# Gaps in the tile of split weights: weights that begin 192 bytes beyond the activations modulo 512

## What is computed

```python
def reference(x, ...):
    x = first_block(x, ln_pre_g, w_in, conv_w, conv_b, w_rg, b_rg, w_ig, b_ig, lru_lambda,
                    w_rnn_out, w_attn_out, w_o, ln_post_g)
    return second_block(x, g_pre_2, w_in_2, ...)

# first block, per layer
    h = rms_norm(x, ln_pre_g[layer])
    proj = jnp.einsum('bsd,de->bse', h, w_in[layer])
    ...
    y = jnp.einsum('bsd,de->bse', merged, w_o[layer])
    x = x + rms_norm(y, ln_post_g[layer])

# second block, per layer
    h = _rmsnorm(x, g_pre)
    u = h @ w_in
    ...
    for n in range(1, N_BRANCH):
        y = y + gates[:, :, n] * (branches[n] @ w_branch[n])
    return y @ w_out
```

## Time and profile before

| | |
|---|---|
| median of 3 runs | 3157.13 us (3156.27 to 3157.97) |
| profiled execution, span from the first to the last instruction | 3154.9 us |
| granted TensorE clock, mean | 0.998 |
| TensorE matmuls | 3134.1 us busy, 99% of the span, 18230 |
| TensorE weight loads | 2741.8 us, 87%, 18230 |
| VectorE | 2130.5 us, 68% |
| ScalarE | 1733.0 us, 55% |
| moved by DMA | 571.67 MB, mean 181 GB/s |

### The profile page before, as it was taken

The page is one execution under the profiler, slowest core; times in us unless marked ns, Lnnn a source line. Parts: engine busy times, 40 slices in busy tenths (PEclk is TensorE's granted clock), DMA queues, the critical chain, the costliest instruction groups (busy, mean ns, idle before and its releaser), DMA issues.

```text
span 3154.9 us, 52176 instructions
## 1 busy us (share of the span) xinstructions
PE 3134.1 (99%) x18230; PEld 2741.8 (87%) x18230; DVE 2130.5 (68%) x2741; ACT 1733.0 (55%) x2291; POOL 0.2 (0%) x4
## 2 busy tenths in 40 slices
PE   9999999999999999999999999999999999999999
PEld 7888888888888788888888888888888888888888
DVE  7677575666667687766666555777776666655575
ACT  5685444444445556656555555645665656555563
POOL 0000000000000000000000000000000000000000
PEclk9999999999999999999999999999999999999999
DMA  7656655555556555565556655566556565665555
GB/s 230 194 168 200 198 187 166 183 177 172 181 167 208 178 168 163 156 198 173 174 171 192 184 181 182 181 198 186 158 157 202 170 179 167 192 189 180 178 185 175
DMA packets 569809, 571.67 MB, mean 181 GB/s; under 512 B 26352, under 2 KB 565488, under 8 KB 569712
## 3 DMA queue, kind: packets, MB, share of 16 engines
q1 hardware_dynamic: 569712, 570.42, 58.9%
HBM read 568.25 MB, written 2.10 MB: 181 GB/s over the span
## 4 chain that ended last, share of the span: by engine, by line
PE 97%; DVE 1%; ACT 1%; DMA 0%; SPq 0%; issue 0%; ACTq 0%; DVEq 0%
PE pg L537 91%; PE pa L771 1%; PE pa L788 1%; PE pa L537 1%; PE pa L778 1%; PE pa L747 1%; PE pa L789 1%; DVE hl L1276 0%; PE pa L704 0%; DMA raw<-w_o 0%; PE pa L878 0%; DMA raw<-w_in 0%; ACT hl L933 0%; SPq L456 0%; DVE uT L1357 0%
## 5 line engine op out<-in xcount | busy, mean ns | idle before, releaser
L537 PE MATMUL pg<-hT,hl 128*128 128x512 f32 x11456 | 2030.6, 337 | 1.1 <-DVE hl L1276 1.1
L537 PEld LDWEIGHTS pg<-hT,hl 128*128 128x128 f32 x11456 | 1750.9, 188 | 261.1 <-DVE hl L1276 4.2
L1276 DVE TENSOR_TENSOR hl<-raw,hl 128x1024 fp32r<-128x1024 f32 (+1 forms) x1071 | 1256.0, 1209 | 314.5 <-ACT hl L933 306.8
L933 ACT ACTIVATE hl<-raw 128x1024 fp32r<-128x1024 f32 (+1 forms) x1071 | 1084.0, 1044 | 313.1 <-PE pg L537 293.8
L537 PE MATMUL pg<-uT,hl 128*128 128x256 f32 (+1 forms) x3712 | 639.1, 333 | 15.9 <-DVE uT L1357 7.5
L537 PEld LDWEIGHTS pg<-uT,hl 128*128 128x128 f32 x3712 | 558.4, 190 | 92.2 <-issue 14.2
L941 ACT ACTIVATE corr<-pg 128x512 f32<-128x512 f32 x286 | 170.3, 596 | 843.0 <-PE pg L537 843.0
L537 PE MATMUL pg<-hl,hT 128*128 128x256 f32 (+1 forms) x1792 | 317.9, 336 | 0.0
L1283 DVE TENSOR_TENSOR work<-pg,corr 128x512 f32<-128x512 f32 (+1 forms) x154 | 105.8, 687 | 303.7 <-ACT corr L941 303.5
L537 PEld LDWEIGHTS pg<-hl,hT 128*128 128x128 f32 x1792 | 274.9, 188 | 40.7
L1283 DVE TENSOR_TENSOR gat<-pg,corr 128x512 f32 (+1 forms) x71 | 48.9, 689 | 139.4 <-ACT corr L941 139.4
(11 more groups left out here) (191 smaller groups left out, 1369.2 us busy)
## 6 DMA issues: line engine op xcount, KB each, us to landing
raw<-w_in SPq DMA_DIRECT2D x791, 512.0 KB, 4.7
raw<-w_br SPq DMA_DIRECT2D x96, 512.0 KB, 4.3
raw<-w_out SPq DMA_DIRECT2D x64, 512.0 KB, 4.7
raw<-w_rnn SPq DMA_DIRECT2D x32, 512.0 KB, 4.8
raw<-w_o SPq DMA_DIRECT2D x32, 512.0 KB, 5.0
raw<-w_att SPq DMA_DIRECT2D x16, 512.0 KB, 4.4
raw<-w_uq SPq DMA_DIRECT2D x16, 384.0 KB, 4.0
tab<-tabs SPq DMA_DIRECT2D x5, 896.0 KB, 7.2
```

The source lines that it names most:

```text
L537: return nc.tensor.matmul(out, lhsT, rhs, start=start, stop=stop, skip_group_check=True)
L933: nc.scalar.activation(hl4[:, j % 2, 0, a:a + n], raw[:, bass.ds(j % 2 * UC + a, n)], ACT.Copy)\
L1276: tt(hl4[:, j % 2, 1, a:a + n], raw[:, bass.ds(j % 2 * UC + a, n)], hl4[:, j % 2, 0, a:a + n].bitcast(F32), ALU.subtract).then_inc(lo_done, 1)
```

## The change

The tile `hl` becomes 224 columns longer (8416 for 8192). In each slot the high part begins 16 columns (64 bytes) in, the low part `UC` columns behind it, and the second slot begins 2 * `UC` + 128 columns behind the first. So all four parts begin 64 bytes beyond the start of `hl` modulo 512. What lies behind `hl` (`hT`, `uT` and all later tiles) moves up by 896 bytes, 384 modulo 512. Relative to the activations in `hT` and `uT` the weights' parts begin at -320, that is 192, bytes modulo 512. Relative to `raw` they begin at 64.

The fixed view `hl4` gives way to a function `part(j, e, h, a, n)`: n columns of slot j, high (e = 0) or low (e = 1) part, half h, from column a. The views that TensorE takes become lists of such slices. The columns taken are the same. Order, shapes and semaphores are the same on every engine: apart from line numbers, the listing of each engine's instructions does not change.

```diff
+HI_AT, LO_AT, SLOT, HL = 16, UC + 16, 2 * UC + 128, 4 * UC + 224
...
-        hl = sb("hl", 4 * UC, F32R)
+        hl = sb("hl", HL, F32R)
...
-        hl4 = hl[:, :].rearrange("p (s h n) -> p s h n", s=2, h=2)
+        def part(j, e, h, a=0, n=UC // 2):
+
+            first = j % 2 * SLOT + (LO_AT if e else HI_AT) + h * UC // 2 + a
+            return hl[:, first:first + n]
+
...
             def split_view(j, n):
 
-                return [hl4[:, j % 2, h, :].rearrange("p (k n) -> p k n", n=n) if UC % n == 0 else
-                        hl4[:, j % 2, h, 0:UC // n * n].rearrange("p (k n) -> p k n", n=n) for h in range(2)]
+                return [[part(j, e, k * n // (UC // 2), k * n % (UC // 2), n) for k in range(UC // n)] for e in range(2)]
...
-                    lambda k, s: mm(pg3[:, b + s, :], wh[:, k - base, s * P:s * P + P], op[:, k, :], start and k == ks[0], False),
-                    lambda k, s: mm(pg3[:, b + s, S:], wl[:, k - base, s * P:s * P + P], op[:, k, 0:S], False,
+                    lambda k, s: mm(pg3[:, b + s, :], wh[k - base][:, s * P:s * P + P], op[:, k, :], start and k == ks[0], False),
+                    lambda k, s: mm(pg3[:, b + s, S:], wl[k - base][:, s * P:s * P + P], op[:, k, 0:S], False,
...
             def apart_view(j, n):
 
-                return [hl4[:, j % 2, h, :].rearrange("p (s n) -> p s n", s=2)[:, :, 0:n] for h in range(2)]
+                return [[part(j, e, h, 0, n) for h in range(2)] for e in range(2)]
 
             def both_view(j, n):
-                return hl4[:, j % 2, :, :].rearrange("p h (k n) -> p k h n", n=n)
+                views = []
+                for k in range(UC // n):
+                    h, a = k * n // (UC // 2), k * n % (UC // 2)
+                    first = j % 2 * SLOT + HI_AT
+                    pair = hl[:, first:first + 2 * (LO_AT - HI_AT)].rearrange("p (e n) -> p e n", e=2)
+                    views.append(pair[:, :, h * UC // 2 + a:h * UC // 2 + a + n])
+                return views
...
                     a = h * UC // 2
-                    nc.scalar.activation(hl4[:, j % 2, 0, a:a + n], raw[:, bass.ds(j % 2 * UC + a, n)], ACT.Copy)\
+                    nc.scalar.activation(part(j, 0, h, 0, n), raw[:, bass.ds(j % 2 * UC + a, n)], ACT.Copy)\
                         .then_inc(hi_done, 1)
...
                     a = h * UC // 2
-                    tt(hl4[:, j % 2, 1, a:a + n], raw[:, bass.ds(j % 2 * UC + a, n)],
-                       hl4[:, j % 2, 0, a:a + n].bitcast(F32), ALU.subtract).then_inc(lo_done, 1)
+                    tt(part(j, 1, h, 0, n), raw[:, bass.ds(j % 2 * UC + a, n)], part(j, 0, h, 0, n).bitcast(F32),
+                       ALU.subtract).then_inc(lo_done, 1)
```

More of the change, by code:

```diff
@@ L575, in token_major @@
                     ks, 2, side,
-                    lambda k, s: mm(pg3[:, b + s, :], op[:, k, s * P:s * P + P], both[:, k - base], start and k == ks[0], False),
-                    lambda k, s: mm(pg3[:, b + s, S:], op[:, k, S + s * P:S + s * P + P], hiw[:, k - base], False,
+                    lambda k, s: mm(pg3[:, b + s, :], op[:, k, s * P:s * P + P], both[k - base], start and k == ks[0], False),
+                    lambda k, s: mm(pg3[:, b + s, S:], op[:, k, S + s * P:S + s * P + P], hiw[k - base], False,
                                     stop and k == ks[-1]))
             def apart_view(j, n):
-                return [hl4[:, j % 2, h, :].rearrange("p (s n) -> p s n", s=2)[:, :, 0:n] for h in range(2)]
+                return [[part(j, e, h, 0, n) for h in range(2)] for e in range(2)]
             def both_view(j, n):
-                return hl4[:, j % 2, :, :].rearrange("p h (k n) -> p k h n", n=n)
+                views = []
[5 more added lines that the diff above has]
+                return views
             def opening(u0, c0, tiles_ready, first_parts, weights_parts=None, summed=None):
@@ L614, in unit @@
                 if form == "r":
-                    wh, wl = (w.rearrange("p h (k n) -> p h k n", n=P) for w in apart_view(j, 512))
+                    wh, wl = ([[w[h][:, k * P:k * P + P] for k in range(4)] for h in range(2)] for w in apart_view(j, 512))
                 for h in halves:
@@ L628, in unit @@
                         if form == "r":
-                            ins = feature_major(b, subs, wh[:, h], wl[:, h], op, ks, begin, end, base + 4 * h, side)
+                            ins = feature_major(b, subs, wh[h], wl[h], op, ks, begin, end, base + 4 * h, side)
                         elif form == "t":
@@ L658, in last_unit_by_bank @@
                     for k in range(8, 16):
-                        mm(pg3[:, 2 + s, :], wh[:, k - 8, col], op[:, k, :], False, False)
-                        ins = mm(pg3[:, 2 + s, S:], wl[:, k - 8, col], op[:, k, 0:S], False, k == 15)
+                        mm(pg3[:, 2 + s, :], wh[k - 8][:, col], op[:, k, :], False, False)
+                        ins = mm(pg3[:, 2 + s, S:], wl[k - 8][:, col], op[:, k, 0:S], False, k == 15)
                     if s == 0:
@@ L799, in queries @@
             def queries(b, u):
-                wh, wl = (w.rearrange("p h (k n) -> p h k n", n=384) for w in apart_view(0, 768))
+                wh, wl = apart_view(0, 768)
                 for out, a in ((pg3[:, b, 0:S], 0), (pg3[:, b, S:], P), (pg3[:, b + 1, 0:S], 2 * P)):
                     for k in range(4):
-                        w = [x[:, k // 2, k % 2, a:a + P] for x in (wh, wl)]
+                        w = [x[k // 2][:, k % 2 * 384 + a:k % 2 * 384 + a + P] for x in (wh, wl)]
                         ins = three_terms(out, *w, u3[:, 8 + k, 0:S], u3[:, 8 + k, S:], k == 0, k == 3)
@@ L812, in keys_and_values @@
                     for k in range(2):
-                        w = [x[:, k, S * e:S * e + P] for x in (wh, wl)]
+                        w = [x[k][:, S * e:S * e + P] for x in (wh, wl)]
                         ins = three_terms(pg3[:, b, e * S:e * S + S], *w, u3[:, 12 + k, 0:S], u3[:, 12 + k, S:], k == 0, k == 1)
                 ins.then_inc(a_part, 1)
-                vh, vl = (w.rearrange("p k (e n) -> p k e n", e=2)[:, :, :, P:S] for w in (wh, wl))
+                vh, vl = ([x.rearrange("p (e n) -> p e n", e=2)[:, :, P:S] for x in w] for w in (wh, wl))
                 for t in range(2):
@@ L819, in keys_and_values @@
                         xh, xl = (u3[:, 12 + k, a + t * P:a + t * P + P] for a in (0, S))
-                        ins = three_terms(pg3[:, b + 1, t * S:t * S + S], xh, xl, vh[:, k], vl[:, k], k == 0, k == 1)
+                        ins = three_terms(pg3[:, b + 1, t * S:t * S + S], xh, xl, vh[k], vl[k], k == 0, k == 1)
                 ins.then_inc(half_done, 2)
@@ L1074, in _ @@
                     act.wait_ge(first_landed, 16)
-                    nc.scalar.activation(hl4[:, 0, 0, 0:512], raw[:, 0:512], ACT.Copy).then_inc(first_hi, 1)
+                    nc.scalar.activation(part(0, 0, 0, 0, 512), raw[:, 0:512], ACT.Copy).then_inc(first_hi, 1)
                 elif n == 1:
                     act.wait_ge(raw_landed[0][0], 16)
-                    nc.scalar.activation(hl4[:, 0, 0, 512:1024], raw[:, 512:1024], ACT.Copy).then_inc(hi_done, 1)
+                    nc.scalar.activation(part(0, 0, 0, 512, 512), raw[:, 512:1024], ACT.Copy).then_inc(hi_done, 1)
                     hi(U_RX, 0, (1,))
@@ L1480, in _ @@
                     dve.wait_ge(first_hi, 1)
-                    tt(hl4[:, 0, 1, 0:512], raw[:, 0:512], hl4[:, 0, 0, 0:512].bitcast(F32), ALU.subtract).then_inc(first_lo, 1)
+                    tt(part(0, 1, 0, 0, 512), raw[:, 0:512], part(0, 0, 0, 0, 512).bitcast(F32), ALU.subtract).then_inc(first_lo, 1)
                 elif n == 1:
                     dve.wait_ge(hi_done, 1)
-                    tt(hl4[:, 0, 1, 512:1024], raw[:, 512:1024], hl4[:, 0, 0, 512:1024].bitcast(F32), ALU.subtract)\
+                    tt(part(0, 1, 0, 512, 512), raw[:, 512:1024], part(0, 0, 0, 512, 512).bitcast(F32), ALU.subtract)\
                         .then_inc(lo_done, 1)
```

## The result

The changed kernel takes 3174.99 us (median of 3 runs, 3173.33 to 3175.02) against 3157.13: the ratio is 1.0055, with a 95% interval of 1.0039 to 1.0071. It is slower by 17.9 us, 0.55%, clear of the noise.

A forecast was written before the change was run, and what follows sets the result against it. TensorE's matmul steps were taken to bound the kernel; 8288 wide plus 8768 narrow products times a price change taken as zero, all else costed at nothing, left 3157 us, with a range of 3090 to 3190 us.

The forecast's parts named there:

- What bounds the kernel: Whole kernel: TensorE, busy 99% of 3154.9 us, sets the time as number of matmuls times step.
- So each matmul costs its columns and about 13.3 ns, wide or narrow: TensorE's float32r products: 346.7 ns a pair split into 226.7 wide and 120.0 narrow, equally 13.3 ns over their columns.
- rival A: Float32r loads beside streams: the price does not look at the address; 3157 us, chance 0.53.
- Everything but the matmuls costs nothing: ScalarE's copies, VectorE's subtractions, DMAs and matrices' views: shifted addresses and moved tiles were costed at nothing.
- I take zero, nearest to the row at 64 bytes: All float32r matmuls: zero price change, as float32 loads from `work` (64 bytes off) and `tab` (on grid) both showed 0.12 us.
- any start meets each phase equally often: Load beside a stream twice as fast: a 512-byte load meets each bank phase equally often wherever it begins, so offset is irrelevant.
- Rival C: Loads beside narrow products: the shift makes load and stream meet more often; 3212 us, or 3175 at a third; chance 0.17.
- bound of 55 us: Worst case from the second block's key rope columns: 353.3 ns a pair, 6.7 more, times 8288 pairs.
- third of it 3175 us: The slower case at a third of the price of the key rope columns: 3175 us.
- Rival B: Loads and streams collide by address and the shift parts them; 46 us gain, 3111 us, chance 0.28.
- bound of 183 us: Best case: shifted loads cost what they cost beside half-rate streams, 11.1 ns less per narrow step, 10.4 per wide.
- 325 ns for a pair: Wide and narrow pair by the skill's N / 2.4 + 2.5 ns; reaching it from 346.7 would bring 180 us.

The follow-up runs named there:

- gaps_no_offset: Changed kernel with its gaps kept but 80 columns fewer behind the parts, so weights and activations begin at the same place modulo 512: 3156.93 us, ratio 1.000.
- steps_by_offset: Kernel of only TensorE's loads and streams, no blocks computed, ten weight offsets in five orders: narrow alone 120.0 ns at offset 0, 113.3 at 64.
- high_192_low_0: Changed kernel with other gaps: high parts 192 bytes beyond the activations modulo 256, low parts at the activations' place: 3123.53 us, ratio 0.9893 to the kernel before.

## Why the prediction was wrong

- **What bounds the kernel**: right. The time is matmuls times step; TensorE's 18.3 us of busy time are the span's 18.2.
- **"So each matmul costs its columns and about 13.3 ns, wide or narrow"**: right for the pair (26.7 ns), not for its halves. The prediction took the narrow step from narrow ones alone and the wide one as the rest. In the window 37.30:85.83 of the kernel before, 140 wide and 140 narrow steps from the matmuls' starts, a wide one takes 231.5 ns and a narrow one 115.2, so 18.2 and 8.5 over their columns. The equal price, on which rival A leaned, was made by the subtraction.
- **Everything but the matmuls costs nothing**: right. gaps_no_offset has the gaps and the moved tiles and takes 3156.93 us (its one execution of 11089.75 us aside); the copies and subtractions keep 1044 and 1209 ns.
- **"I take zero, nearest to the row at 64 bytes"**: this is the step that failed. The sum was 17056 matmuls times the change of the price, and that change is not zero: it is some 1.1 ns on the mean (18.2 us over 17056), 1.7 in turn. The price looks at the address: with narrow products alone, a float32r step is 113.3 ns at 64 bytes against 120.0 at 0. The earlier trace rows compared two single float32 loads, each behind one float32r product, in places where the step was whatever the pattern before had made it. One step of 0.12 us, read to 0.01, could not carry this, and 64 bytes is not the offset of the change, 192. The earlier trace rows did not either: a latency beside which no load ran can hold its own load's lateness, as the text itself said.
- **Rival A's argument, that any start meets each phase equally often**: falls with it, since the step does depend on the address. It counts meetings as if one did not move the next. The several steady steps at one offset suggest that each does; this is an argument, not shown.
- **Rival C, slower**: this is what happened, given 0.17. Its bound of 55 us came from the earlier trace rows, 176.7 ns, and 176.7 is indeed the step that in-turn work takes in the changed kernel's second product; its "third of it 3175 us" is the result, by luck of the mixture. Taking every matmul's step in both traces and sorting by the order around it, the work in turn (11165 steps, 173.5 to 175.2 ns where nothing interrupts it) grew by 17.8 us and the values in turn (1448) by 4.5; two and two (3010) fell by 3.3 us and narrow ones alone (533) by 2.5; all others grew by 1.8. Together that is 18.3 us, the loss in the span. Its mechanism was half right. It put the price on the load beside a narrow product, and narrow ones alone became cheaper (120.0 to 117.8 or 113.3). What became dearer is the alternation. And the earlier trace rows need not be another placement: 176.7 is the second step in turn at offset 0. Whether its one bank matters was not tried.
- **Rival B, faster**: wrong for this pair of offsets, right about the place. The part of the 26.7 ns that an offset can give back is 6.7 (340.0 instead of 346.7 a pair), a quarter, as guessed; it takes unlike offsets for high and low. The bound of 183 us was never near: 20 of the 26.7 ns stood in every steady order measured.
- **The chances**: 0.28 for faster is rival B alone; with the 0.01 that the text adds to it, it would be 0.29.
- **The Trainium skill**: "SBUF — State Buffer", section "Who interferes with whom", says that TensorE's two read ports are independent and that it never waits on anyone. By that the offset is worth nothing. steps_by_offset, with no other engine at work, shows steps from 113.3 to 120.0 ns for the same narrow products at different offsets. The measurement decides; that the read ports are the place is not shown. The prediction's 325 ns for a pair came from the Trainium skill's "TensorE: Matmul & The Clock Gate", section "Back-to-back issue gap", whose formula is for a matmul taken by itself. No pair in any steady stretch here took under 340.0 ns.

The range 3090 to 3190 held the time, since it was built from the bounds; 0.19 for slower was too little. The row that should have counted for more was the earlier trace rows: equal widths and order, and 6.7 ns a pair dearer, in one and the same trace. It told that the step is not fixed by the shapes.

## What to carry to other kernels

When a kernel is one unbroken chain of matmuls, read the step, not the latency, in each stretch of one order; two stretches of the same shapes and order with different steps say that placement, or the pattern that a stretch has settled into, matters, and a percent or so may lie there. Measure it with a kernel of nothing but loads and streams over offsets, orders and several starts before choosing a layout, then try the few best in the real kernel: here high parts 192 bytes and low parts 0 beyond the activations took 3123.53 us, 1.1% under the kernel before, with no instruction added. Do not work out one kind's step in one order from its step in another. Judge an order and an offset together, and look again at both after any edit ahead of them, since a stretch can settle into a dearer pattern. What was tried here is one kernel's sizes on one core.

## What the runs showed of the hardware

- The step of float32r matmuls, each with a load of 128 weights of its own, depends on where the weights begin relative to the activations: wide alone 226.6 to 233.4 ns, narrow alone 113.3 to 120.0 (steps_by_offset). Four pairs of offsets 256 bytes apart agree in every order. Finer than 64 bytes counts too (16 bytes: narrow alone 118.3 for 120.0, two and two 176.7 for 174.2).
- At high 192, low 0 in turn the pattern is the simplest and the cheapest seen: in high_192_low_0 wide steps take 227 ns and narrow ones 113 (the trace counts whole ns), as little as the least seen alone, 226.6 and 113.3. At 2.4 GHz 340.0 ns are 816 clock periods, 48 over the 768 columns; the pairs of 346.7, 350.0 and 353.3 ns have 64, 72 and 80 over them.
- Plain float32 matmuls take the same in every kernel, 0.98 us for nine transposes. But their operands (`work`, `cst`) lie behind `hl` and moved together, so no run tells whether an offset would matter to them.
- Steady steps come back at the same values (170.0, 172.5, 173.3, 174.2, 175.0, 176.7 ns a matmul above all; others between them occur), and a stretch can stay at its value for hundreds of matmuls with all engines at work: 280 steps at 170.0 ns with a DMA share of 0.65. After a delay of some 20 ns one stretch at offset 0 went on at 176.7 instead of 173.3.
- What inside TensorE or its reads makes the pattern was not tried and stays open. So do which single load of the pair pays, and whether the output banks play a part.
